# Attention scores from split operands, and the last two weight blocks in token order with the final norm on VectorE

## The chip, the cores and the metric

One NeuronCore of a Trainium2 chip runs the whole program in one launch. It has five engines with a queue each: TensorE (PE: matmuls; PEld: its weight loads), VectorE (DVE), ScalarE (ACT), GpSimd (POOL) and SyncE (SP, which here only issues transfers). The time is the device time of one execution in microseconds, given as the median of several runs.

## The reference

Two transformer layers over 1024 tokens of width 1024, all in float32. The first (`first_block`) mixes gated linear attention, a second recurrence and cross attention; the change doesn't touch it. The second (`second_block`) is where the change lies:

```python
h = x @ w_in[i]
ua, va, za, qh, kh, vh, zb, ga, gb = jnp.split(h, IN_OFFSETS, axis=-1)
...
q = apply_rope(qh.reshape(bn, s_len, B_HEADS, 2, B_QK_DIM), cos, sin) * (B_QK_DIM ** -0.5)
k = apply_rope(kh.reshape(bn, s_len, B_HEADS, 2, B_QK_DIM), cos, sin)
...
sc = jnp.einsum("bqhmd,bkhmd->bhmqk", qblk, k)          # 8 heads, 2 maps m, 64 wide
pr = jax.nn.softmax(jnp.where(mask, sc, -jnp.inf), axis=-1)
a = pr[:, :, 0] - lam * pr[:, :, 1]
o = jnp.einsum("bhqk,bkhd->bqhd", a, v)
...
merged = jax.nn.sigmoid(ga) * (ya @ w_branch_a[i]) + jax.nn.sigmoid(gb) * (yb @ w_branch_b[i])
mix_out = merged @ w_out[i]
x = layer_norm(DEEPNORM_ALPHA * x + mix_out + ple, ln_g[i], ln_b[i])
```

## The kernel before

The program is written by hand, engine by engine: each has a list of stages (`p0_..` to `p9_..`), and semaphores order the engines. Every large product is made from split operands: a value is stored as a high part (`at_hi`, `w_hi`, type float32r, a copy on ScalarE) and a low part (`at_lo`, `w_lo`, the difference, on VectorE or GpSimd), and three matmuls high x high, low x high, high x low add up in a PSUM bank. Weights come as 84 blocks of 256 columns; ScalarE makes `w_hi` of a block (`split_high`, line 390), GpSimd `w_lo` (`split_low`, line 377). A block has four tiles. In form F (lines 411 to 413) a tile is 128 features by 512 tokens, in form T (lines 422 to 424) it is two groups of 128 tokens by 256 columns, 48 matmuls. A quarter of a tile is a part (`gemm_part`).

The stages that matter here:

- Stage 5 ends with the rotation tables, the rotation of q (VectorE) and k (GpSimd) of head 0 in three steps each (`rope_third`), and the last block before the attention. All engines but TensorE then meet at `phase_end(5)`, which an engine leaves only when the others have come.
- Stage 8 is the differential attention, 8 heads with 8 query blocks of 128 tokens each (`head_pe`, `head_act`, `head_dve`, `head_pool`). For block qb TensorE computes the scores of block qb+1 in two PSUM areas, `ps_a` for map 0 and `ps_b` for map 1 (`attention_scores`, line 2480, keys in pieces of at most 512); VectorE adds the mask and takes the maximum (`scores_max`), ScalarE the exponential (line 2415), VectorE combines the maps into `da` (line 2277), TensorE transposes it (line 2447), ScalarE copies it to `daT` (line 2384), TensorE multiplies with v (line 2458). Between these steps TensorE works off 48 parts per head of other products, laid out in slots (`SLOT_PARTS`): 5 in `FIRST_SLOT`, 2 or 3 in front of the wait for `da`, and so on, 3 in `LAST_SLOT`. The first scores of the next head come behind the last product with v and before `LAST_SLOT` (`first_scores`). The scores are plain float32 products of the rotated q and k, map 0 on partitions 0 to 63 and map 1 on 64 to 127; q and k are double-buffered over heads (`dqx[head % 2]`), and SP loads those of the next head at the start of a head (`queries_load`). The rotation for the next head runs at query blocks 2 to 4.
- Stage 9 merges the branches and ends with `gemm_last`, two segments of two T blocks. Their tiles are added to `X` by VectorE (`sum_tile`, line 580, and `last_sum`, line 1774): block 0 for all four tiles (token pairs), then block 1. With the second segment's second block token pairs become complete one by one, and the final norm runs per group of 128 tokens: statistics of two halves (line 2844) and aggregation (line 2846) on VectorE, variance to 1/root on GpSimd (`root`, lines 300 and 302), the bias (line 2851) on VectorE, scale and bias on ScalarE (line 2792), gain on VectorE (line 2858), shift on GpSimd, or on VectorE for groups 5 and 7 (`last_shift`, line 2874), and the store by SP.

## Time and profile before

| | |
|---|---|
| time, median of 3 runs | 2433.26 us (2432.01 to 2437.83) |
| profiled execution | 2439.78 us, of it span 2437.9 us |
| TensorE busy | 2362.6 us, 97% |
| VectorE busy | 1290.5 us, 53% |
| ScalarE busy | 907.1 us, 37% |
| GpSimd busy | 792.2 us, 32% |
| TensorE's granted clock | full in nearly all slices |

The span runs from the first to the last recorded instruction. A matmul's recorded duration includes its way through the array, so records overlap; how fast TensorE works is read from the distance between two starts. The attention stage lies between 1372 and 2097 us of the span, the last block's tiles from 2366 us on.

### The profile page before, as it was taken

Reading aid. Unit: us, or ns where it says so; the run is one execution under the profiler, and the core shown is the slowest. Engines: PE = TensorE matmul, PEld = TensorE weight load, DVE = VectorE, ACT = ScalarE, POOL = GpSimd, SP = SyncE. Lnnn points to the kernel's source line nnn. Section 1 sums busy time; section 2 is a strip of 40 time slices with the busy share of each in tenths; the row PEclk is TensorE's granted clock in tenths of the full one; section 3 lists DMA queues with packets and bytes.
Section 4 is the critical chain, followed back from the end, with each engine's and each line's share of the span. In section 5 each row is a group of like instructions: output and inputs, shape, how many; then the busy total and the mean of one; then the engine's idle time right before and its main releaser. Section 6 shows DMA issues by size and latency. Waiting matters only on the chain.

```text
span 2437.9 us, 38783 instructions
## 1 busy us (share of the span) xinstructions
PE 2362.6 (97%) x15376; PEld 2042.5 (84%) x15376; DVE 1290.5 (53%) x2614; ACT 907.1 (37%) x1669; POOL 792.2 (32%) x712
## 2 busy tenths in 40 slices
PE   8999999999999999999999999999999999999995
PEld 7879978798788899999888898777898777887795
DVE  4002359999997433271323546446446446577626
ACT  4124554444444432242222333333333334544311
POOL 3111324445543221222443333233233232331123
PEclk9999999999999999999999999999999999999998
DMA  6234334443334522133334524314324314566611
GB/s 257 74 112 159 119 143 140 130 147 110 117 104 149 207 96 79 53 122 104 105 105 125 174 70 147 113 70 147 114 69 147 113 70 178 181 225 216 207 52 70
DMA packets 138940, 311.98 MB, mean 128 GB/s; under 512 B 12288, under 2 KB 55936, under 8 KB 127504
## 3 DMA queue, kind: packets, MB, share of 16 engines
q1 hardware_dynamic: 80080, 223.62, 26.8%
q10 hardware_dynamic: 58688, 86.00, 9.9%
q8 instruction: 116, 1.90, 0.3%
q14 instruction: 56, 0.46, 0.1%
HBM read 211.54 MB, written 98.04 MB: 127 GB/s over the span
## 4 chain that ended last, share of the span: by engine, by line
PE 86%; DVE 7%; issue 2%; POOL 1%; ACT 1%; DMA 1%; POOLq 0%; SPq 0%; ACTq 0%; DVEq 0%
PE bank L411 12%; PE bank L413 11%; PE bank L412 11%; PE bank L422 9%; PE bank L423 9%; PE bank L424 9%; PE bank L2480 3%; PE bank L2458 3%; PE bank L1842 3%; PE bank L1843 3%; PE bank L1841 3%; PE bank L1460 2%; PE bank L2447 1%; PE bank L730 1%; PE bank L2765 1%
## 5 line engine op out<-in xcount | busy, mean ns | idle before, releaser
L411 PE MATMUL bank<-at_hi,w_hi 128*128 128x512 f32 x1408 | 582.7, 414 | 2.6 <-DVE stage L2007 0.9
L422 PE MATMUL bank<-w_hi,at_hi 128*128 128x256 f32 x1920 | 556.8, 290 | 0.5 <-issue 0.5
L413 PE MATMUL bank<-at_hi,w_lo 128*128 128x512 f32 x1408 | 552.8, 393 | 0.0
L412 PE MATMUL bank<-at_lo,w_hi 128*128 128x512 f32 x1408 | 551.3, 392 | 0.0
L424 PE MATMUL bank<-w_hi,at_lo 128*128 128x256 f32 x1920 | 544.4, 284 | 0.0
L423 PE MATMUL bank<-w_lo,at_hi 128*128 128x256 f32 x1920 | 544.3, 283 | 0.0
L377 POOL TENSOR_TENSOR w_lo<-w_raw,w_hi 128x2048 fp32r<-128x2048 f32 x70 | 322.9, 4613 | 626.4 <-ACT w_hi L390 602.3
L422 PEld LDWEIGHTS bank<-w_hi,at_hi 128*128 128x128 f32 x1920 | 370.0, 193 | 13.2 <-issue 11.8
L423 PEld LDWEIGHTS bank<-w_lo,at_hi 128*128 128x128 f32 x1920 | 369.5, 192 | 0.7 <-issue 0.2
L424 PEld LDWEIGHTS bank<-w_hi,at_lo 128*128 128x128 f32 x1920 | 369.0, 192 | 0.0
L411 PEld LDWEIGHTS bank<-at_hi,w_hi 128*128 128x128 f32 x1408 | 268.9, 191 | 75.7 <-issue 23.3
L300 POOL TENSOR_TENSOR small<-small,cols 128x1 f32<-128x1 f32 (+1 forms) x162 | 54.9, 339 | 806.5 <-ACT da_junk L2399 439.4
L413 PEld LDWEIGHTS bank<-at_hi,w_lo 128*128 128x128 f32 x1408 | 265.5, 189 | 58.8
L412 PEld LDWEIGHTS bank<-at_lo,w_hi 128*128 128x128 f32 x1408 | 266.6, 189 | 51.9 <-issue 3.6
L447 ACT ACTIVATE stage<-bank 128x512 f32<-128x512 f32 x232 | 138.0, 595 | 441.4 <-PE bank L413 299.9
L390 ACT ACTIVATE w_hi<-w_raw 128x2048 fp32r<-128x2048 f32 x70 | 134.0, 1914 | 140.6 <-PE bank L424 104.9
L302 POOL TENSOR_TENSOR small<-small,cols 128x1 f32<-128x1 f32 (+1 forms) x162 | 146.5, 905 | 12.7
L2310 DVE SCALAR_TENSOR_TENSOR da_y<-bank,da_lam,da_gate 128x128 f32<-128x128 f32 x64 | 22.4, 350 | 236.5 <-PE bank L2468 236.5
L2384 ACT ACTIVATE da_aT<-bank 128x512 f32<-128x512 f32 (+2 forms) x96 | 47.1, 491 | 197.2 <-PE bank L2447 189.7
L2322 DVE TENSOR_REDUCE small<-bank 128x1 f32<-128x256 f32 (+7 forms) x128 | 97.1, 758 | 4.3
L2415 ACT ACTIVATE da_p<-bank,small 128x256 f32<-128x256 f32 (+7 forms) x128 | 93.2, 737 | 0.6 <-DVE small L2324 0.5
L1237 POOL TENSOR_TENSOR rec_z<-rec_z,rec_k 128x128 f32<-128x128 f32 x128 | 79.8, 624 | 25.9 <-ACT rec_z L1207 25.4
(300 smaller groups left out, 3606.7 us busy)
## 6 DMA issues: line engine op xcount, KB each, us to landing
w_raw<-in_weights SPq DMA_DIRECT2D x84, 1024.0 KB, 7.6
feat<-stage ACTq DMA_DIRECT2D x184, 256.0 KB, 2.0
tok<-stage ACTq DMA_DIRECT2D x72, 256.0 KB, 2.1
stage<-feat SPq DMA_DIRECT2D x32, 256.0 KB, 3.5
w_mem<-in_w_mem SPq DMA_DIRECT2D x4, 1024.0 KB, 7.5
x<-in_x SPq DMA_DIRECT2D x4, 1024.0 KB, 11.4
logg<-gate_g ACTq DMA_DIRECT2D x8, 512.0 KB, 2.8
rec_b<-logg SPq DMA_DIRECT2D x16, 256.0 KB, 5.1
```

Source lines behind the costliest of these rows:

```text
L302: pool.tensor_tensor(to, to, cols[:, ROOT:ROOT + 1].broadcast_to(shape), ALU.pow).then_inc(sem_, 1)
L377: pool.tensor_tensor(w_lo[b][:], w_raw[:, b, :, :], w_hi[b][:].bitcast(F32), ALU.subtract).then_inc(w_split, 1)
L390: nc.scalar.activation(w_hi[b][:], w_raw[:, b, :, :], ACT.Copy).then_inc(w_high, 1)
L411: nc.tensor.matmul(ps_gemm[i % 2], wh, ah, start=(k == 0), stop=False)
L412: nc.tensor.matmul(ps_gemm[i % 2], wh, al, start=False, stop=False)
L413: last = nc.tensor.matmul(ps_gemm[i % 2], wl, ah, start=False, stop=(k == KT - 1))
L422: nc.tensor.matmul(o, ah, wh, start=(k == 0), stop=False)
L423: nc.tensor.matmul(o, ah, wl, start=False, stop=False)
L424: last = nc.tensor.matmul(o, al, wh, start=False, stop=(k == KT - 1))
L447: nc.scalar.activation(stage[:, i, :], ps_gemm[i % 2], s.func, scale=s.scale).then_inc(tile_out, 1)
L2322: nc.vector.reduce_max(small[:, m:m + 1], flat, AX.X).then_inc(d_x, 1)
L2415: nc.scalar.activation(dp[:, m, 0:n], scored(ps, qb), ACT.Exp, bias=small[:, 2 + m:3 + m], scale=DSCALE, accum_out=small[:, 4 + m:5 + m]). ...
```

## The change

In the attention, q and k are split as the operands of the large products are. The rotated q and k are held once (`dqx`, `dkx`, no longer by head parity); ScalarE copies them to `dqh`, `dkh` (`queries_high`) and VectorE writes the differences `dql`, `dkl` (`queries_low`). For head 0 this is at the end of stage 5, for the others in query block 7 of the head before, behind ScalarE's last copies to `daT` and behind VectorE's norm of block 6. TensorE's first scores of a head, and SP's loads of the next q and k, wait for the differences. Head 0 runs its `FIRST_SLOT` ahead of its first scores. The scores of a piece of keys are six products: high x high, high x low, low x high, each for map 0 and then map 1.

At the end, the two blocks of the last segment are computed in the order of `LAST_TILES`, so that token pairs are finished one after another. The low part of the last weight block is made by VectorE. Statistics are taken over 256 columns, those of the first three quarters as soon as a pair's first tile is added. The norm is two VectorE passes: (x - mean) x gain, then x 1/root + shift; ScalarE's pass, the bias and GpSimd's shifts are gone.

```diff
         def queries_load(sp, head):
 
             row = head * P
-            if head >= 2:
-                sp.wait_ge(d_s, (head - 1) * 16 + 1)
             if head:
-                sp.wait_ge(d_rq, 3 * head)
-                sp.wait_ge(d_rk, 3 * head)
-            for x, swapped, at, done in ((dqx[head % 2], dqs, QF + row, d_in), (dkx[head % 2], dks, KF + row, d_in)):
+                sp.wait_ge(d_low, LOWS_BEFORE + 2 * head)
+            for x, swapped, at, done in ((dqx, dqs, QF + row, d_in), (dkx, dks, KF + row, d_in)):
...
+        def queries_high(act, head):
+
+            act.wait_ge(d_s, head * 16 + 1)
+            for hi, x, ready in ((dqh, dqx, d_rq), (dkh, dkx, d_rk)):
+                act.wait_ge(ready, 3 * head + 3)
+                nc.scalar.activation(hi[:], x[:], ACT.Copy).then_inc(d_high, 1)
+
+        def queries_low(dve, head):
+
+            for n, (lo, hi, x) in enumerate(((dql, dqh, dqx), (dkl, dkh, dkx))):
+                dve.wait_ge(d_high, HIGHS_BEFORE + 2 * head + n + 1)
+                nc.vector.tensor_tensor(lo[:], x[:], hi[:].bitcast(F32), ALU.subtract).then_inc(d_low, 1)
...
                     scores_max(dve, it, qb + 1)
+                elif not last_head:
+                    queries_low(dve, it + 1)
...
                     attention_exp(act, it, qb + 1)
+                elif it < B_HEADS - 1:
+                    queries_high(act, it + 1)
...
         def p8_pe(pe):
+            slot_products(pe, 0, FIRST_SLOT)
             first_scores(pe, 0)
...
         def first_scores(pe, it):
 
-            pe.wait_ge(d_rq, 3 * it + 3)
-            pe.wait_ge(d_rk, 3 * it + 3)
+            pe.wait_ge(d_low, LOWS_BEFORE + 2 * it + 2)
...
         def attention_scores(pe, it, qb):
             n = (qb + 1) * P
-            for m, ps in enumerate((ps_a, ps_b)):
-                if qb >= LONG:
-                    pe.wait_ge(d_e, it * 16 + (2 * qb + m + 1))
-                elif qb >= 2:
-                    pe.wait_ge(d_e, it * 16 + (2 * (qb - 1) + m + 1))
-                rows = slice(m * DK, (m + 1) * DK)
-                for a in range(0, n, HALF):
-                    w = min(HALF, n - a)
-                    last = nc.tensor.matmul(scored(ps, qb)[:, a:a + w], dqx[it % 2][rows, qb * P:(qb + 1) * P],
-                                            dkx[it % 2][rows, a:a + w],
-                                            start=True, stop=True)
-                last.then_inc(d_s, 1)
+            if qb >= LONG:
+                pe.wait_ge(d_e, it * 16 + (2 * qb + 2))
+            elif qb >= 2:
+                pe.wait_ge(d_e, it * 16 + (2 * (qb - 1) + 2))
+            for a in range(0, n, HALF):
+                w = min(HALF, n - a)
+                for i, (q, k) in enumerate(((dqh, dkh), (dqh, dkl), (dql, dkh))):
+                    for m, ps in enumerate((ps_a, ps_b)):
+                        rows = slice(m * DK, (m + 1) * DK)
+                        last = nc.tensor.matmul(scored(ps, qb)[:, a:a + w], q[rows, qb * P:(qb + 1) * P], k[rows, a:a + w],
+                                                start=(i == 0), stop=(i == 2))
+                        if i == 2 and a + w == n:
+                            last.then_inc(d_s, 1)
...
+            gemm_pe(pe, gemm_last[:1], lambda k, h: FILLED3 + (4 + h) * KT + k)
+            for n in range(len(LAST_TILES)):
+                last_tile(pe, n)
+
+        LAST_TILES = ((0, 0), (0, 1), (1, 0), (1, 1), (0, 2), (1, 2), (0, 3), (1, 3))
...
+            dve.wait_ge(w_split, gemm_last[1].first + 3)
+            split_low(dve, gemm_last[1].first // 2, 1)
+            for n, (b, i) in enumerate(LAST_TILES):
+                final_sum(dve, n)
+                for t in (2 * i, 2 * i + 1):
+                    if b:
+                        link(dve, statistics(t, 3))
+                        nc.vector.bn_aggr(lst[:, t, 0:2], lst[:, t, 4:28]).then_inc(l_var, 1)
+                    else:
+                        for part in range(3):
+                            statistics(t, part)
+                if b:
+                    for t in (2 * i, 2 * i + 1):
+                        centred(dve, t)
+                    for t in (2 * i, 2 * i + 1):
+                        normalized(dve, t)
...
+        def centred(dve, t):
+
             if t == 0:
                 dve.wait_ge(bc_in, 48)
-            nc.vector.tensor_tensor(X[:, t, :], X[:, t, :], bc[:, 0, :], ALU.mult).then_inc(l_g, 1)
+            dve.wait_ge(l_var, t + 1)
+            nc.vector.scalar_tensor_tensor(X[:, t, :], X[:, t, :], lst[:, t, 0:1], bc[:, 0, :], ALU.subtract,
+                                           ALU.mult).then_inc(l_g, 1)
+
+        def normalized(dve, t):
+
+            dve.wait_ge(l_g, t + 1)
+            dve.wait_ge(l_root, 2 * t + 2)
+            nc.vector.scalar_tensor_tensor(X[:, t, :], X[:, t, :], lst[:, t, 2:3], bc[:, 1, :], ALU.mult,
+                                           ALU.add).then_inc(l_out, 1)
```

## Rows read from the trace of the kernel before

**Rows 1.** The page: the span, and the chain that ended last by engine.

```profile
span 2437.9 us, 38783 instructions
PE 86%; DVE 7%; issue 2%; POOL 1%; ACT 1%; DMA 1%; POOLq 0%; SPq 0%; ACTq 0%; DVEq 0%
```

**Rows 2.** Timeline of the end: start, us, engine, line, count [idle before]; VectorE, then GpSimd.

```profile
2372.35 0.69 DVE L1774 TENSOR_TENSOR X<-bank,X 128x512 f32<-128x512 f32 x1 [5.07 <-PE bank L424]
...
2395.39 0.69 DVE L1774 TENSOR_TENSOR X<-bank,X 128x512 f32<-128x512 f32 x1 [5.07 <-PE bank L424]
2396.11 1.29 DVE L2844 BATCH_NORM_STATS2 lst<-X 128x6 f32<-128x512 f32 x2
2397.44 0.21 DVE L2846 BATCH_NORM_AGGREGATE lst<-lst 128x2 f32<-128x12 f32 x1
...
2418.91 0.68 DVE L1774 TENSOR_TENSOR X<-bank,X 128x512 f32<-128x512 f32 x1
...
2429.02 2.35 DVE L2858 TENSOR_TENSOR X<-X,bc 128x1024 f32<-128x1024 f32 x2
2431.40 3.25 DVE L2874 TENSOR_TENSOR X<-X,bc 128x1024 f32<-128x1024 f32 x1
...
2430.31 3.25 POOL L2874 TENSOR_TENSOR X<-X,bc 128x1024 f32<-128x1024 f32 x1 [3.62 <-DVE X L2858]
```

**Rows 3.** Timeline of a head's change and of three score blocks, TensorE and VectorE.

```profile
1640.81 1.95 PE L2458 MATMUL bank<-da_v,da_aT 128*128 128x128 f32 x16
1642.69 0.49 PE L2480 MATMUL bank<-da_k,da_q 64*128 64x128 f32 x4
...
1655.56 0.35 DVE L2277 SCALAR_TENSOR_TENSOR da_a<-da_p,small 128x128 f32<-128x128 f32 x1
...
1657.91 0.27 PE L2447 MATMUL bank<-ident,da_a 128*128 128x128 f32 x1
...
1668.44 1.13 PE L2480 MATMUL bank<-da_k,da_q 64*128 64x512 f32 x4
1669.50 0.50 PE L411 MATMUL bank<-at_hi,w_hi 128*128 128x512 f32 x1
...
1708.95 1.99 PE L2480 MATMUL bank<-da_k,da_q 64*128 64x512 f32 x8
1710.87 0.50 PE L411 MATMUL bank<-at_hi,w_hi 128*128 128x512 f32 x1
```

**Rows 4.** Timeline of TensorE where the attention stage begins.

```profile
1369.70 0.39 PE L411 MATMUL bank<-at_hi,w_hi 128*128 128x512 f32 x1
...
1371.52 0.39 PE L413 MATMUL bank<-at_hi,w_lo 128*128 128x512 f32 x1
...
1377.95 0.28 PE L424 MATMUL bank<-w_hi,at_lo 128*128 128x256 f32 x1
...
1379.76 0.28 PE L424 MATMUL bank<-w_hi,at_lo 128*128 128x256 f32 x1
...
1383.88 0.33 PE L2447 MATMUL bank<-ident,da_a 128*128 128x128 f32 x1
```

**Rows 5.** Timeline of ScalarE: two passes of 1024 columns, and a head's last copy.

```profile
1353.49 1.04 ACT L2357 ACTIVATE da_cos<-da_cos 128x1024 f32<-128x1024 f32 x1
1354.44 1.04 ACT L2357 ACTIVATE da_sin<-da_sin 128x1024 f32<-128x1024 f32 x1
...
1638.14 0.60 ACT L2384 ACTIVATE da_aT<-bank 128x512 f32<-128x512 f32 x1 [1.22 <-PE bank L2447]
```

**Rows 6.** Timeline of GpSimd and VectorE where the attention stage begins.

```profile
1374.99 4.62 POOL L377 TENSOR_TENSOR w_lo<-w_raw,w_hi 128x2048 fp32r<-128x2048 f32 x1 [7.68 <-ACT w_hi L390]
...
1379.71 0.30 DVE L2320 TENSOR_TENSOR bank<-bank,causal 128x128 f32<-128x128 f32 x1 [11.31 <-POOLq L290]
```

**Rows 7.** Stretches of TensorE around a fall of its clock: busy, granted clock, DMA share.

```profile
1026.00:1028.40 2.40, 1.73 (x12) 1.00 0.00 0
1028.40:1031.80 3.40, 3.40 (x18) 0.50 0.00 0
```

More of the change, by code:

```diff
@@ L216, in build @@
         with ExitStack() as own:
[L217 to L219 removed]
+            dqs, dks, dcos, dsin, dqx, dkx = [sb(f"da_{n}", [P, TOK], F32, own) for n in ("qs", "ks", "cos", "sin", "q", "k")]
+            dqh, dql, dkh, dkl = [sb(f"da_{n}", [P, TOK], F32R, own) for n in ("q_hi", "q_lo", "k_hi", "k_lo")]
             dv = [sb(f"da_v{n}", [P, NT, P], F32, own) for n in range(2)]
@@ L2768, in p9_pe, with last_tile @@
                     last.then_inc(e_prod, 1)
-            gemm_pe(pe, gemm_last, lambda k, h: FILLED3 + (4 + h) * KT + k)
+            gemm_pe(pe, gemm_last[:1], lambda k, h: FILLED3 + (4 + h) * KT + k)
+            for n in range(len(LAST_TILES)):
+                last_tile(pe, n)
+        LAST_TILES = ((0, 0), (0, 1), (1, 0), (1, 1), (0, 2), (1, 2), (0, 3), (1, 3))
+        def last_tile(pe, n):
+            g, (b, i) = gemm_last[1].first, LAST_TILES[n]
+            if i == 0:
+                pe.wait_ge(w_split, g + b + 3)
+            pe.wait_ge(tile_out, 4 * g + n + 1)
+            for j in range(2):
+                tok = slice((2 * i + j) * P, (2 * i + j + 1) * P)
+                o = ps_gemm[n % 2][:, j * CB:(j + 1) * CB]
+                for k in range(KT):
+                    wh, wl, ah, al = w_hi[b][:, k, :], w_lo[b][:, k, :], at_hi[:, k, tok], at_lo[:, k, tok]
+                    nc.tensor.matmul(o, ah, wh, start=(k == 0), stop=False)
+                    nc.tensor.matmul(o, ah, wl, start=False, stop=False)
+                    last = nc.tensor.matmul(o, al, wh, start=False, stop=(k == KT - 1))
+            last.then_inc(tile_done, 1)
         def p9_act(act):
@@ L2837, in merge, with final_sum, statistics @@
             nc.vector.scalar_tensor_tensor(x, x, ALPHA, e, ALU.mult, ALU.add).then_inc(e_out, 1)
-        POOL_SHIFTS = [t for t in range(NT) if t not in (NT - 3, NT - 1)]
-        def last_statistics(dve, t):
-            for n in range(2):
-                last = nc.vector.bn_stats(lst[:, t, 4 + 6 * n:10 + 6 * n], X[:, t, n * HALF:(n + 1) * HALF])
-            link(dve, last)
-            nc.vector.bn_aggr(lst[:, t, 0:2], lst[:, t, 4:16]).then_inc(l_var, 1)
-        def last_bias(dve, t):
-            dve.wait_ge(l_root, 2 * t + 2)
-            nc.vector.scalar_tensor_tensor(lst[:, t, 3:4], lst[:, t, 0:1], -1.0, lst[:, t, 2:3], ALU.mult,
-                                           ALU.mult).then_inc(l_nb, 1)
-        def last_gain(dve, t):
-            dve.wait_ge(l_x, t + 1)
+        def final_sum(dve, n):
+            g, (b, i) = gemm_last[1].first, LAST_TILES[n]
+            dve.wait_ge(tile_done, 4 * g + n + 9)
+            x = X[:, 2 * i:2 * i + 2, (2 + b) * CB:(3 + b) * CB]
+            nc.vector.tensor_tensor(x, ps_gemm[n % 2].rearrange("p (t n) -> p t n", t=2), x, ALU.add).then_inc(tile_out, 1)
+            dve.wait_ge(tile_out, 4 * g + n + 3)
+        def statistics(t, n):
+            return nc.vector.bn_stats(lst[:, t, 4 + 6 * n:10 + 6 * n], X[:, t, n * CB:(n + 1) * CB])
+        def centred(dve, t):
             if t == 0:
                 dve.wait_ge(bc_in, 48)
-            nc.vector.tensor_tensor(X[:, t, :], X[:, t, :], bc[:, 0, :], ALU.mult).then_inc(l_g, 1)
+            dve.wait_ge(l_var, t + 1)
[6 more added lines that the diff above has]
+                                           ALU.add).then_inc(l_out, 1)
         def p9_pool(pool):
             low_of(pool, gemm_a)
-            low_of(pool, gemm_last)
+            split_low(pool, gemm_last[1].first // 2, 0)
             for t in range(NT):
@@ L2865, in p9_pool @@
                 root(pool, lst[:, t, 2:3], lst[:, t, 1:2], E2, l_root, 2 * t + 1)
-                if t % 2 and t > 2:
-                    for before in (t - 3, t - 2):
-                        if before in POOL_SHIFTS:
-                            last_shift(pool, before, l_out)
-            last_shift(pool, NT - 2, l_out)
-        def last_shift(eng, t, done):
-            eng.wait_ge(l_g, t + 1)
-            eng.tensor_tensor(X[:, t, :], X[:, t, :], bc[:, 1, :], ALU.add).then_inc(done, 1)
         block = ctx.enter_context(nc.Block())
```

49 lines of the change are left out of this document (14 added, 35 removed).

## The prediction

> **What bounds the kernel now.** I read the page first. The chain that ended last is 86% TensorE and 7% VectorE, of a span of 2437.9 us [rows 1]. So almost everywhere a microsecond of TensorE's queue is a microsecond of time; the VectorE share has to be looked for in one place. The timeline of the last stretch shows where: TensorE's tiles of the last block arrive every 5.76 us (2372.35 to 2395.39 is four steps), so the eighth of them is due at 2412.67, but the span ends 25 us later. In between VectorE is behind: it takes the eighth tile only at 2418.91, and its last instruction ends at 2434.65 [rows 2]. Then I read TensorE's timeline around the scores, which are what the change rewrites there, and at last the places where the new instructions go: the start of the attention stage and the end of a head.
>
> **Part 1, the scores' products.** Before, each score product is a full f32 one and leaves two matmul records (four for two maps). For a block of queries with 512 and with 1024 keys, TensorE's next work starts 1.06 and 1.92 us after the first of them [rows 3]. That is 1.67 ns per key for both maps (0.86 us over 512 keys), or four columns' time at 2.4 GHz, plus a fixed 0.21. In the same stretch a full-array f32 product of 128 columns costs two records of 0.117 (16 in 1.88 us), also about four cycles per column, for one product. Two maps at the price of one: their products, on rows 0 to 63 and 64 to 127 of the array, already run side by side, although the program issues map 0 entirely before map 1. "The two maps in turn" therefore buys nothing that isn't there; what it must do is keep it.
>
> After, each piece of keys takes three passes of split operands per map instead of one f32 product. The price of such a pass is that of the other split products: 512 columns 0.2275 (1369.70 to 1371.52, eight steps), 256 columns 0.1207 (1377.95 to 1379.76, fifteen steps) [rows 4]; 384 columns lie between, 0.174. For 128 columns no row shows one. The f32 record of 128 columns takes 0.117, and the 256-column pass 0.1207, so I take 0.12. A head has pieces of 512 six times, and of 384, 256 and 128 twice each: 3 x (6 x 0.2275 + 2 x 0.174 + 2 x 0.1207 + 2 x 0.12) = 6.6 us. Before it was 4608 keys x 1.67 ns = 7.7. That is 1.1 a head, 8.8 us in eight. The side-by-side passes have less between them than the full-array ones (0.43 for 512 columns at two cycles each, which is 0.003 over the arithmetic, against 0.014 over it); with that the new passes cost 6.15, and the gain is 12.2. I take 10. The fixed 0.21 stays. No wait takes the gain back: at the block shown here VectorE's probabilities are ready at 1655.91 and TensorE transposes them at 1657.91 [rows 3], and the scores shorten a block by 0.36 us at most. The wait for both maps' exponentials instead of one is none, as both maps' passes already started together.
>
> **Part 2, the splits at a head's end.** ScalarE gets two copies of 1024 columns behind its last copy of transposed probabilities, VectorE two subtractions behind them, and TensorE's first scores of the next head wait for both. From rows: the copy ends at 1638.74, a ScalarE pass over 1024 columns takes 1.04 and the next starts 0.95 later, so the second ends at about 1640.8; a VectorE pass over 1024 takes 1.22 (two in 2.35), so the second difference ends at about 1642.3. TensorE's first score product began at 1642.69 [rows 3, 5]. I cost it at nothing, with a cover of 0.3 us: TensorE's products beside it. If the cover is missed by half a microsecond, seven heads cost 3.5, and by a whole VectorE pass 8.5. Behind the waiting instructions, ScalarE's eviction of a product tile moves by 1.2 us (its bank is next needed one tile, some 5 us, later), and VectorE's gate of the block before by about as much; TensorE asks for that only after its next three parts. The loads for the next head wait for the differences instead of the rotations, which end before the loads' place in SP's queue comes (behind the store of the head's outputs). The copies of q and k that are no longer double cost nothing for the same reason.
>
> **Part 3, the first head.** Here the cover is too short. ScalarE's weight split, for which GpSimd's w_lo pass waits, ends at 1374.9, the two new copies at about 1377. VectorE's differences then meet GpSimd's w_lo pass, 1374.99 to 1379.61 [rows 6]. Two such passes do not share: beside a GpSimd pass of 3.25 us a VectorE pass takes 3.25 where one alone takes 1.2, and ends when the other is done and its own 1.1 is over [rows 2]. So the differences run from 1379.6 to 1382.0. TensorE, with the first slot's five parts now ahead of the scores, starts them at 1371.75 and ends 60 x 0.1207 later, at 1379.0, and stands for 3 us. Before, VectorE began on the first scores when GpSimd was through the stage's end, at 1379.71, and TensorE's first transpose was at 1383.88, 4.17 later [rows 4, 6]. Now it begins at about 1382.6, and the transpose comes at 1386.8: +2.9 us. A standstill of this size may also drop the clock: in the rows at 1026 to 1032 TensorE has been busy 72% of the time before, and then runs 3.4 us at the 1.2 GHz level [rows 7]. That loses 1.7, of which the wait for the probabilities would hide some. I add 0.5. Bounds: +1.5 (the difference gets in before GpSimd) and +5.
>
> **Part 4, the end.** The order of the last eight tiles becomes (0,0) (0,1) (1,0) (1,1) (0,2) (1,2) (0,3) (1,3). A pair of token tiles is complete with its second block: at tiles 3, 4, 6 and 8, not 5 to 8. TensorE's work is the same; the second block's weights are wanted two tiles earlier, 11.5 us behind a split of 2048 columns, two passes of 1.04 on ScalarE and two of 1.14 on VectorE, so nothing waits. Statistics over 512 columns take 0.65 each (1.29 for two), over 256 I take 0.40 (between half and all of it). A first-block tile is 0.72 for the sum and six statistics, 2.9. A second-block tile is 0.72, two statistics and two aggregations (0.21 each) [rows 2] 1.2, and four passes over 1024 columns of 1.14: 6.5, with a wait for GpSimd's root behind VectorE's passes 6.75. Queue: tile 3 is due at 2383.87 and done at 2390.6, tile 4 at 2397.4, tile 5 at 2400.3, tile 6 (due 2401.15) at 2407.9, tile 7 at 2410.8, before tile 8 at 2412.67. So the end is 2412.67 + 6.75 = 2419.4, and with what follows VectorE's last instruction now (2437.9 - 2434.65 = 3.25, the last store), 2422.7. Gain 15.2 us. If the root holds up each pair by 1.1 and the short statistics cost as much as the long ones, VectorE is behind again and the gain is 10; with none of that 15.7. ScalarE's scaling and GpSimd's shift, whose passes now block VectorE's [rows 2], go away: they were part of the chain, not beside it.
>
> **Sum.** -10 - 15.2 + 2.9 + 0.5 = -21.8 us. The profiled execution took 2439.78 (span 2437.9 and 1.9 around it), 0.3% over the median of 2433.26; by its own time it becomes 2418.0, and the median 2411.5.
>
> **The rivals.** (a) Slower: the passes of the two maps don't run side by side at one column per cycle. All pairs in this trace do it at two cycles per column; at twice the rate both maps read and write together, which nothing here shows. Then each pair costs two passes: 13.2 us a head instead of 7.7, +44 in all, and the kernel ends at 2433.3 + 44 - 11.8 = 2465. It decides from the point where scores cost 12 us more than now, a pair at 1.4 passes. For it: no row. Against it: the exact four cycles per key. 6%.
>
> (b) Each pass shows its weight load. The fixed 0.21 says that a load is exposed where the array changes between its full and its split use; if half of it, 0.107, were paid at every pass, 36 passes a head would add 3.85 us to the 5.8 of their columns (three times 4608 at 2.4 GHz): 9.6 against 7.7, +15 in all, 2433.3 + 15.5 - 11.8 = 2437, no change. Against it: from 512 to 1024 keys two passes more cost 0.86, no load among them [rows 3]. 3%. The Trainium skill, "TensorE: Matmul & The Clock Gate", Part 3, says that weight loads overlap with matmuls in flight only when the row group differs; by that rule it would be this case, and the trace disagrees. The same page has matmuls start strictly in program order, under which the maps could not have overlapped before; the 1.67 ns per key disagree with that too.
>
> (c) Passes of 128 columns cost four cycles a column, 0.21 instead of 0.12: 48 of them, +4.6, 2416. Nothing in the trace speaks against it. 10%.
>
> (d) The splits at a head's end come late, by half to a whole VectorE pass in seven heads: 2415 to 2420. The cover is only 0.3 us. 13%.
>
> (e) VectorE stays behind at the end: gain 10, 2416.7. 8%.
>
> **Chances.** The forecast 60%. (c), (d) and (e) lie between 2415 and 2420, 31%; (a) 6%, (b) 3%. Range: forecast with gains of 8.8 to 12.2 and 13 to 15.7, a first head of +1.5 to +5, and the spread of the runs shown (2432.0 to 2437.8), reaches from 2405 to 2416; with (c) to (e) to 2421. A difference of 0.3%, 7.3 us, is about what can be told from no change here. Faster by more: 0.91; within: 0.03; slower: 0.06.
>
> **What would show it.** After: score blocks of 128, 512 and 1024 keys span about 0.57, 0.89 and 1.57 us; the first scores of head 0 start near 1382, those of the next heads directly behind the products before; VectorE's last tile is taken at its due time and the span ends 10 us behind the last matmul. The prediction is wrong if 512-key blocks take over 1.5 us (a), if TensorE stands before each head's first scores (d), or if the eighth tile waits for VectorE (e).

## The result, and the profile after

The changed kernel takes 2414.28 us (median; 2410.88 to 2414.99) against 2433.26: the ratio is 0.9917, with an interval of 0.9902 to 0.9932. Run once more on another chip it took 2412.51, a ratio of 0.9902 (0.9888 to 0.9915). The forecast was 2411.5. One execution of the kernel before took 5162.6 us and is in none of these numbers.

The page of the changed kernel: the span, the busy times, and the chain that ended last by engine, to be laid beside [rows 1].

```profile
span 2409.1 us, 39201 instructions
...
PE 2350.1 (98%) x15568; PEld 2055.7 (85%) x15568; DVE 1315.2 (55%) x2645; ACT 911.0 (38%) x1677; POOL 775.0 (32%) x705
...
PE 88%; DVE 8%; issue 1%; DMA 1%; ACT 1%; POOL 0%; ACTq 0%; DVEq 0%; SPq 0%
```

The spans of the two profiled executions differ by 28.8 us, more than the medians (19.0). 5.7 of it lies where both kernels are the same: the last product ahead of the attention starts at 1371.52 in the one and at 1365.85 in the other. That point moves from run to run, also in the kernels below (1360.4 to 1368.3), because short stretches at half clock fall now here, now there in the stages before: eight of them, 30.7 us in all, ahead of the attention in the run before, and four, 20.5 us in all, in the one after. Half of such a stretch is lost, so they account for some 5 of the 5.7. So I measure from it. From there to the end of the span it is 1066.4 us before, 1043.2 after, and 1043.9 in the other profiled run of the changed kernel. The change's own gain is 22.5 to 23.2 us. This table splits it; each number is a difference of two starts on TensorE, the last of a start and the span's end.

| stretch | before | after | difference | forecast |
|---|---|---|---|---|
| last product ahead of the attention to first transpose | 12.36 | 15.72 | +3.4 | +2.9 + 0.5 |
| first transpose to last product with v | 713.5 | 703.1 | -10.4 | -10 |
| from there to the last matmul | 315.0 | 314.2 | -0.8 | 0 |
| last matmul to the span's end | 25.56 | 10.25 | -15.3 | -15.2 |

**The scores.** TensorE's timeline in the changed kernel around score blocks of head 1: 128 keys (its first scores), 512 keys, the second piece (128 keys) of the block of 640, and 1024 keys. L2498 is the new scores; the row behind the blocks of 128, 512 and 1024 keys is TensorE's next work.

```profile
1457.46 0.33 PE L2498 MATMUL bank<-da_k_hi,da_q_hi 64*128 64x128 f32 x2
1457.62 0.27 PE L2498 MATMUL bank<-da_k_lo,da_q_hi 64*128 64x128 f32 x2
1457.73 0.27 PE L2498 MATMUL bank<-da_k_hi,da_q_lo 64*128 64x128 f32 x2
1457.94 0.39 PE L421 MATMUL bank<-w_hi,at_hi 128*128 128x256 f32 x1
...
1484.01 0.50 PE L2498 MATMUL bank<-da_k_hi,da_q_hi 64*128 64x512 f32 x2
...
1484.90 0.39 PE L421 MATMUL bank<-w_hi,at_hi 128*128 128x256 f32 x1
...
1492.70 0.23 PE L2498 MATMUL bank<-da_k_hi,da_q_hi 64*128 64x128 f32 x2
1492.76 0.28 PE L2498 MATMUL bank<-da_k_lo,da_q_hi 64*128 64x128 f32 x2
...
1523.84 0.49 PE L2498 MATMUL bank<-da_k_hi,da_q_hi 64*128 64x512 f32 x2
1524.17 0.39 PE L2498 MATMUL bank<-da_k_lo,da_q_hi 64*128 64x512 f32 x2
...
1525.42 0.51 PE L410 MATMUL bank<-at_hi,w_hi 128*128 128x512 f32 x1
```

The blocks span 0.48, 0.89 and 1.58 us; 512 and 1024 keys took 1.06 and 1.92 [rows 3]. Each row is a pair of passes, one for each map (x2), mostly 3 to 10 ns apart. Over the eight blocks of a head it is now 0.48, 0.55, 0.72, 0.90, 1.17, 1.24, 1.43, 1.59, sum 8.08 us; before it was 0.42, 0.63, 0.85, 1.06, 1.29, 1.50, 1.71, 1.92, sum 9.38. The difference, 1.30, is 10.4 us in eight heads.

**The first head.** The changed kernel at the start of the attention: timelines of ScalarE, GpSimd, VectorE, then TensorE, and then TensorE's granted clock in three stretches (busy, granted clock, DMA share).

```profile
1370.09 1.04 ACT L2187 ACTIVATE da_k_hi<-da_k 128x1024 fp32r<-128x1024 f32 x1
...
1369.32 4.63 POOL L376 TENSOR_TENSOR w_lo<-w_raw,w_hi 128x2048 fp32r<-128x2048 f32 x1 [8.13 <-ACT w_hi L389]
...
1370.22 4.81 DVE L2193 TENSOR_TENSOR da_q_lo<-da_q,da_q_hi 128x1024 fp32r<-128x1024 f32 x1 [7.94 <-ACT da_q_hi L2187]
1374.95 1.21 DVE L2193 TENSOR_TENSOR da_k_lo<-da_k,da_k_hi 128x1024 fp32r<-128x1024 f32 x1
1376.87 0.30 DVE L2333 TENSOR_TENSOR bank<-bank,causal 128x128 f32<-128x128 f32 x1 [0.71 <-PE bank L2498]
...
1376.22 0.33 PE L2498 MATMUL bank<-da_k_hi,da_q_hi 64*128 64x128 f32 x2 [2.31 <-DVE da_k_lo L2193]
...
1381.57 0.27 PE L2464 MATMUL bank<-ident,da_a 128*128 128x128 f32 x1
```

```profile
1374.00:1376.20 2.20, 0.00 (x0) 1.00 0.00 0
1376.20:1378.10 1.90, 1.88 (x20) 1.00 0.44 106
1378.10:1381.50 3.40, 3.40 (x18) 0.50 1.04 296
```

VectorE's first difference is ready to run at 1370.22, but GpSimd has been in its weight pass since 1369.32. The difference is recorded at 4.81 us instead of 1.2 and ends 1.08 behind GpSimd's end (1373.95). The second follows, and TensorE stands 2.3 us. TensorE does nothing from 1374.0 to 1376.2, works for 1.9 us at full clock, and then for 3.4 us at half clock (1.2 GHz), as in the rows at 1028 [rows 7].

**A head's end.** ScalarE and VectorE in the changed kernel, the end of head 0.

```profile
1452.79 0.60 ACT L2398 ACTIVATE da_aT<-bank 128x512 f32<-128x512 f32 x1 [1.26 <-PE bank L2464]
1453.29 1.05 ACT L2187 ACTIVATE da_q_hi<-da_q 128x1024 fp32r<-128x1024 f32 x1
1454.23 1.05 ACT L2187 ACTIVATE da_k_hi<-da_k 128x1024 fp32r<-128x1024 f32 x1
...
1455.51 1.22 DVE L2193 TENSOR_TENSOR da_k_lo<-da_k,da_k_hi 128x1024 fp32r<-128x1024 f32 x1
```

The second difference ends at 1456.73, 0.73 us ahead of TensorE's first scores (1457.46). The distance from TensorE's last product with v to these scores is 0.205, as before, in all seven heads: nothing stands.

**The end.** VectorE and GpSimd from the last-but-one tile on, and TensorE's last matmul, in the changed kernel.

```profile
2394.32 0.68 DVE L2876 TENSOR_TENSOR X<-bank,X 128x512 f32<-128x512 f32 x1
2395.03 2.06 DVE L2881 BATCH_NORM_STATS2 lst<-X 128x6 f32<-128x256 f32 x6
2399.16 0.69 DVE L2876 TENSOR_TENSOR X<-bank,X 128x512 f32<-128x512 f32 x1 [2.07 <-PE bank L2803]
...
2401.11 2.41 DVE L2888 SCALAR_TENSOR_TENSOR X<-X,lst,bc 128x1024 f32<-128x1024 f32 x2
2403.44 2.48 DVE L2895 SCALAR_TENSOR_TENSOR X<-X,lst,bc 128x1024 f32<-128x1024 f32 x2
...
2402.45 1.48 POOL L301 TENSOR_TENSOR lst<-lst,cols 128x1 f32<-128x1 f32 x1
...
2398.84 0.28 PE L2803 MATMUL bank<-w_hi,at_lo 128*128 128x256 f32 x1
```

VectorE has been idle for 2.07 us when the last tile comes; before, it took its last tile 6.2 us late [rows 2]. From there it needs 6.75 us (2399.16 to 2405.91), and the store 3.2 more: 10.0 us from taking the last tile to the end, where it was 19.0 (2418.91 to 2437.9). So of the 15.3 us some 6 are the lateness and 9 the work behind the last tile. In the kernel before, the tile taken at 2410.07 kept VectorE for 8.85 us, and its longest part is an operation on one column per partition:

```profile
2415.57 2.29 DVE L2851 SCALAR_TENSOR_TENSOR lst<-lst 128x1 f32<-128x1 f32 x1 [0.71 <-POOL lst L302]
```

This is the bias. It takes 0.11 where GpSimd is idle (at 2413.62), and here it ends with GpSimd's shift pass (2415.50 to 2417.84). The new norm has neither.

### The profile page after: what moved, and what is told of

It is laid out like the page before. It is cut to its first block, busy times and chain, and to the rows that moved or that the text cites. A ratio compares the mean times of both kernels' runs of the same rounds, so it can differ in the third digit from the quotient of the medians.

```text
span 2409.1 us, 39201 instructions
## 1 busy us (share of the span) xinstructions
PE 2350.1 (98%) x15568; PEld 2055.7 (85%) x15568; DVE 1315.2 (55%) x2645; ACT 911.0 (38%) x1677; POOL 775.0 (32%) x705
## 3 DMA queue, kind: packets, MB, share of 16 engines
q8 instruction: 117, 1.92, 0.3%
## 4 chain that ended last, share of the span: by engine, by line
PE 88%; DVE 8%; issue 1%; DMA 1%; ACT 1%; POOL 0%; ACTq 0%; DVEq 0%; SPq 0%
PE bank L410 12%; PE bank L412 12%; PE bank L411 12%; PE bank L421 9%; PE bank L422 8%; PE bank L423 8%; PE bank L2498 3%; PE bank L2475 3%; PE bank L1841 3%; PE bank L1840 3%; PE bank L1842 3%; PE bank L2464 1%; PE bank L1459 1%; PE bank L729 1%; PE bank L2780 1%
## 5 line engine op out<-in xcount | busy, mean ns | idle before, releaser
L421 PE MATMUL bank<-w_hi,at_hi 128*128 128x256 f32 x1792 | 521.1, 291 | 0.8 <-issue 0.8
L423 PE MATMUL bank<-w_hi,at_lo 128*128 128x256 f32 x1792 | 508.8, 284 | 0.0
L422 PE MATMUL bank<-w_lo,at_hi 128*128 128x256 f32 x1792 | 508.6, 284 | 0.0
L421 PEld LDWEIGHTS bank<-w_hi,at_hi 128*128 128x128 f32 x1792 | 345.9, 193 | 8.9 <-issue 7.1
L422 PEld LDWEIGHTS bank<-w_lo,at_hi 128*128 128x128 f32 x1792 | 345.6, 193 | 0.7 <-issue 0.2
L423 PEld LDWEIGHTS bank<-w_hi,at_lo 128*128 128x128 f32 x1792 | 345.1, 193 | 0.0
L410 PEld LDWEIGHTS bank<-at_hi,w_hi 128*128 128x128 f32 x1408 | 268.0, 190 | 64.7 <-issue 12.5
L299 POOL TENSOR_TENSOR small<-small,cols 128x1 f32<-128x1 f32 (+1 forms) x162 | 52.7, 326 | 795.6 <-ACT da_junk L2415 431.4
L301 POOL TENSOR_TENSOR small<-small,cols 128x1 f32<-128x1 f32 (+1 forms) x162 | 124.1, 766 | 12.7
L1236 POOL TENSOR_TENSOR rec_z<-rec_z,rec_k 128x128 f32<-128x128 f32 x128 | 95.2, 744 | 26.4 <-ACT rec_z L1206 26.0
```

The lines of the kernel that those rows point to most:

```text
L301: pool.tensor_tensor(to, to, cols[:, ROOT:ROOT + 1].broadcast_to(shape), ALU.pow).then_inc(sem_, 1)
L410: nc.tensor.matmul(ps_gemm[i % 2], wh, ah, start=(k == 0), stop=False)
L421: nc.tensor.matmul(o, ah, wh, start=(k == 0), stop=False)
L422: nc.tensor.matmul(o, ah, wl, start=False, stop=False)
L423: last = nc.tensor.matmul(o, al, wh, start=False, stop=(k == KT - 1))
L1236: eng.tensor_tensor(z1, z1, k1, ALU.mult)
```

## The experiments

Times are medians. "Changed" means the kernel after the change. Stretches are read as in the table above. The intervals of the changed kernel's own two ratios reach from 0.9888 to 0.9932. Experiments 4 and 7 to 10 have ratios within them, so the times alone don't tell these kernels from the changed one, and only the stretches show what each does.

**1. Only the scores' part.** The edit undoes everything in the last stage; these are its main lines:

```diff
-            gemm_pe(pe, gemm_last[:1], lambda k, h: FILLED3 + (4 + h) * KT + k)
-            for n in range(len(LAST_TILES)):
-                last_tile(pe, n)
+            gemm_pe(pe, gemm_last, lambda k, h: FILLED3 + (4 + h) * KT + k)
...
-                    for t in (2 * i, 2 * i + 1):
-                        centred(dve, t)
-                    for t in (2 * i, 2 * i + 1):
-                        normalized(dve, t)
```

> The kernel before with the change's scores alone: split operands, passes of the maps in turn, the first slot ahead of head 0's scores; the end is that of before. My theory (parts add up): 10.3 us less in the attention, 3.4 us more at head 0, so 7 us less than before, about 2426.5; 25.5 us from the last matmul to the end as before. Rival (the parts interact, or the scores' gain is given back by the end): within 3 us of before.

2425.0 us, ratio 0.9973 (0.996 to 0.9986) to the kernel before (2431.93 on this chip): -7. First transpose to last product with v takes 702.9 us, and last matmul to end 25.6, as before the change.

**2. Only the end.** The reverse: the attention is that of the kernel before.

```diff
-            pe.wait_ge(d_low, LOWS_BEFORE + 2 * it + 2)
+            pe.wait_ge(d_rq, 3 * it + 3)
+            pe.wait_ge(d_rk, 3 * it + 3)
...
-            slot_products(pe, 0, FIRST_SLOT)
```

> The kernel before with the change's end alone. My theory: the last matmul to the end goes from 25.6 us to 10.3, the attention is as before, so 15.3 us less, about 2418. Together with the scores alone it gives the whole change, 22 us. Rival: the end's gain depends on when weights or constants arrive, and is under 12 us without the earlier attention.

2418.72 us, ratio 0.9934 (0.9914 to 0.9954), or -13. The trace gives the size better: last matmul to end takes 10.25 us (-15.3), the attention's stretch 713.8. The two parts are additive: -7 and -13 timed make 20, and the two traces give -10.6 for the attention's stretch, +2.8 ahead of it and -15.3, which is -23.1.

**3. The two maps one after the other.**

```diff
-            for a in range(0, n, HALF):
-                w = min(HALF, n - a)
-                for i, (q, k) in enumerate(((dqh, dkh), (dqh, dkl), (dql, dkh))):
-                    for m, ps in enumerate((ps_a, ps_b)):
-                        rows = slice(m * DK, (m + 1) * DK)
+            for m, ps in enumerate((ps_a, ps_b)):
+                rows = slice(m * DK, (m + 1) * DK)
+                for a in range(0, n, HALF):
+                    w = min(HALF, n - a)
+                    for i, (q, k) in enumerate(((dqh, dkh), (dqh, dkl), (dql, dkh))):
```

> The changed kernel, but each block's scores are issued with all of map 0's passes first and then all of map 1's. My theory: TensorE runs the two row halves side by side whatever the order of issue (the f32 scores of before, issued map by map, cost 1.67 ns per key for both), so score blocks span the same 0.48, 0.90 and 1.59 us and the time is that of the changed kernel within 3 us. Rival (matmuls start in the order of issue, so that the alternation is what brings the overlap): with a block's three or six passes of a map in a row only one neighbouring pair overlaps; a 512-key block goes from 0.90 to about 1.35 us or more, a head from 8.1 us of scores to about 13, and the time is 35 to 45 us longer, about 2455.

2430.35 us, ratio 0.9987 (0.9977 to 0.9996). Neither theory gave this. Blocks of up to 512 keys are unchanged (0.90 for 512); those of two pieces take 1.74, 1.82, 2.00 and 2.18 instead of 1.17 to 1.59, and the stretch of the attention is 722.0 us, 18.9 longer. TensorE's timeline of a block of 1024 keys in this kernel:

```profile
1529.95 0.50 PE L2498 MATMUL bank<-da_k_hi,da_q_hi 64*128 64x512 f32 x1
1530.30 0.40 PE L2498 MATMUL bank<-da_k_lo,da_q_hi 64*128 64x512 f32 x1
1530.54 0.39 PE L2498 MATMUL bank<-da_k_hi,da_q_lo 64*128 64x512 f32 x1
1530.54 0.62 PE L2498 MATMUL bank<-da_k_hi,da_q_hi 64*128 64x512 f32 x2
...
1531.58 0.39 PE L2498 MATMUL bank<-da_k_lo,da_q_hi 64*128 64x512 f32 x1
1531.81 0.39 PE L2498 MATMUL bank<-da_k_hi,da_q_lo 64*128 64x512 f32 x1
1532.14 0.50 PE L410 MATMUL bank<-at_hi,w_hi 128*128 128x512 f32 x1
```

The first two passes run alone. The third (high k, low q) has a high x high pass beside it, 7 ns later. It is 0.228 ahead of the next one of map 0, so it must be on the other half of the rows: map 1's first, the seventh in TensorE's queue. It starts when the third does and did not start with the first or second. At the other end map 1's last two passes (from 1531.58 on) run alone. So TensorE starts a pass ahead of its turn: from four places ahead (the seventh with the third), but not from five or six (with the second or the first). It is the same in all 32 blocks of two pieces: the seventh pass starts 0.57 to 0.59 us behind the first. As the first three passes are 512 columns wide in all of them, no run here tells a reach counted in places from one counted in time.

The Trainium skill, "TensorE: Matmul & The Clock Gate", Part 3, says that matmuls start in program order without exception; the trace disagrees, as the seventh starts 0.23 us ahead of the fourth. The same section says that small products on distinct groups of rows start about 4 ns apart; here the distances are mostly 3 to 10 ns.

**4. The maps apart within each piece.** If the reach is four places, nothing should be lost with the maps three passes apart instead of six.

```diff
-                for i, (q, k) in enumerate(((dqh, dkh), (dqh, dkl), (dql, dkh))):
-                    for m, ps in enumerate((ps_a, ps_b)):
-                        rows = slice(m * DK, (m + 1) * DK)
+                for m, ps in enumerate((ps_a, ps_b)):
+                    rows = slice(m * DK, (m + 1) * DK)
+                    for i, (q, k) in enumerate(((dqh, dkh), (dqh, dkl), (dql, dkh))):
```

> The changed kernel, but within each piece of keys map 0's three passes come first and then map 1's three. With the maps apart over the whole block (six passes each where there are two pieces) blocks of over 512 keys went from 1.59 to 2.18 us, those of one piece (three passes each) did not. My theory: TensorE starts a pass of the other row half ahead of its turn if it stands at most four places behind the passes in progress; here it stands three behind, so all blocks span what they do in the changed kernel (0.90 and 1.59 us for 512 and 1024 keys), and the time is within 3 us of it. Rival (what matters is that the two pieces differ in bank, or that a second piece cannot start ahead of the first): blocks of two pieces stay at about 2.2 us and the time at about 2430.

2410.01 us, ratio 0.9901 (0.9886 to 0.9916); the changed kernel on the same chip has 0.9902. The attention's stretch is 703.7 us. A block of 1024 keys in this kernel:

```profile
1518.47 0.50 PE L2498 MATMUL bank<-da_k_hi,da_q_hi 64*128 64x512 f32 x2
1518.81 0.40 PE L2498 MATMUL bank<-da_k_lo,da_q_hi 64*128 64x512 f32 x2
...
1520.07 0.51 PE L410 MATMUL bank<-at_hi,w_hi 128*128 128x512 f32 x1
```

All are pairs again and the block spans 1.59. Map 1's first pass, the fourth in the queue, starts 10 ns behind the first. Three places ahead is in reach, four is by experiment 3, and five isn't.

**5. The kernel before, with its maps in turn.** The old f32 products, two per map, are issued piece by piece.

```diff
-            for m, ps in enumerate((ps_a, ps_b)):
...
-                for a in range(0, n, HALF):
-                    w = min(HALF, n - a)
+            for a in range(0, n, HALF):
+                w = min(HALF, n - a)
+                for m, ps in enumerate((ps_a, ps_b)):
```

> The kernel before, with its plain f32 score products issued in turn for the two maps within each piece of keys, and the wait for both maps' exponentials in front, as in the change. My theory: an f32 product is two passes, so map by map the other map's first pass stands at most four behind, and all of it already overlaps: no change, within 3 us of before, blocks of 1024 keys at 1.92 us. Rival (the wait for both exponentials costs something, or the turn gains something for f32 too): over 3 us either way.

2435.53 us, ratio 1.0003 (0.9993 to 1.0013), and blocks of 0.42 to 1.92 us as before. In the kernel before, map 1's first product was the third in the queue at most. It leaves two records to a product, so its first record is the fifth, four places behind the first, and starts 13 to 14 ns after it. By either count that is within the reach of experiment 3: turns buy nothing there.

**6. The splits at a head's end one tile later.**

```diff
-                elif it < B_HEADS - 1:
-                    queries_high(act, it + 1)
...
+                if it < B_HEADS - 1 and qb == NT - 1:
+                    queries_high(act, it + 1)
```

> The changed kernel with ScalarE's two split copies of a head's end issued after the eviction of the product tile instead of before it, about 1.3 us later. In the changed kernel the second difference ends 0.73 us before the next head's first scores start. My theory: the cover is about 0.5 to 0.7 us, so TensorE stands 0.6 to 0.8 us before the first scores of seven heads, 4 to 6 us in all, about 2419. Rival (the wait is covered more widely, TensorE's queue hides it): no change within 2 us.

2421.15 us, ratio 0.9948 (0.993 to 0.9966). The attention's stretch is 713.4 us: the whole gain of the scores is gone. ScalarE at the end of head 0 in this kernel, then TensorE's first scores of head 1:

```profile
1452.33 0.60 ACT L2398 ACTIVATE da_aT<-bank 128x512 f32<-128x512 f32 x1 [1.27 <-PE bank L2464]
1453.76 0.60 ACT L446 ACTIVATE stage<-bank 128x512 f32<-128x512 f32 x1 [0.84 <-PE bank L423]
1454.39 0.37 ACTq L456 DMA_DIRECT2D tok<-stage  x1
1455.16 1.06 ACT L2187 ACTIVATE da_q_hi<-da_q 128x1024 fp32r<-128x1024 f32 x1 [0.80 <-ACT stage L446]
...
1458.66 0.33 PE L2498 MATMUL bank<-da_k_hi,da_q_hi 64*128 64x128 f32 x2 [1.60 <-DVE da_k_lo L2193]
```

The copies begin 2.83 us behind the start of the last copy to `daT`, where they began 0.50 behind it. The eviction is not 0.6 us of work but a wait for the tile (0.84), the pass, and 0.80 from the pass's end to the next pass, in which the transfer is issued (0.37). The first scores then start 1.59 us behind the last product with v (1.87 in head 1, for which this row stands) instead of 0.205. 2.3 later costs 1.4 per head: the cover was 0.9 us.

**7. The first head's high parts ahead of the last weight split.**

```diff
                 for i in range(4):
                     evacuate(act, s, 0, b, i)
+                    if (b, i) == (1, 2):
+                        queries_high(act, 0)
...
-            queries_high(act, 0)
```

> The changed kernel with ScalarE's copies of head 0's q and k issued two evictions earlier, right behind the rotation, so that VectorE's differences are over before GpSimd's last w_lo pass of the stage begins. TensorE's first slot still stands ahead of the scores. My theory (the standstill at head 0 comes from VectorE's difference waiting for GpSimd's pass): TensorE's gap of 2.6 us before the first scores goes, and with it the 3.4 us at half clock; from the last product of the stage before to the first transpose it takes 13.6 to 14.5 us instead of 15.7, as VectorE still takes the scores only after the stage's end; time 1.5 to 2 us less, about 2412.5. Rival (the cause is the stage's end, or the order of ScalarE's queue): the gap stays.

2411.14 us, ratio 0.9915 (0.99 to 0.993; the kernel before had 2432.63 on this chip). VectorE and GpSimd in this kernel:

```profile
1364.59 1.22 DVE L2193 TENSOR_TENSOR da_q_lo<-da_q,da_q_hi 128x1024 fp32r<-128x1024 f32 x1 [1.19 <-ACT da_q_hi L2187]
1365.73 1.22 DVE L2193 TENSOR_TENSOR da_k_lo<-da_k,da_k_hi 128x1024 fp32r<-128x1024 f32 x1
...
1369.86 4.61 POOL L376 TENSOR_TENSOR w_lo<-w_raw,w_hi 128x2048 fp32r<-128x2048 f32 x1 [7.54 <-ACT w_hi L389]
```

Ahead of GpSimd's pass both differences take 1.22 each. TensorE doesn't stand (gap of 0.21), its clock stays full, and the last product to the first transpose takes 12.8 us instead of 15.7, less than the 13.6 expected. From VectorE's first score pass to the transpose it is 4.17 us, as before the change, against 4.70 in the changed kernel, so 0.5 of the changed kernel's 3.4 us are clock; experiments 1, 3 and 9, without the fall of the clock, have 15.2. From 15.2 to 12.8, 2.4 us, is the price of meeting GpSimd. The 0.5 that are left against 12.36 come from the first slot: TensorE starts the scores only behind it, 8.0 us after the last product, and VectorE gets them at 8.65, where it began at 8.19 in the kernel before.

**8. The same, with the first scores ahead of `FIRST_SLOT` again.**

```diff
         def p8_pe(pe):
-            slot_products(pe, 0, FIRST_SLOT)
             first_scores(pe, 0)
```

> The same with head 0's first scores ahead of the first slot again, as in the kernel before. My theory: the first transpose comes 12.3 us after the last product of the stage before, as in the kernel before (12.36), so 3.4 us less than the changed kernel: about 2411. Rival: ScalarE's early copies delay the eviction of a tile and TensorE stands for them, no gain.

2410.24 us, ratio 0.9914 (0.99 to 0.9928). The stretch is 12.5 us, with a gap of 1.08 in front of the scores, as the second difference ends late (1366.62). In experiment 10, which starts the attention the same way, it ends in time, the gap is 0.65 as in the kernel before, and the stretch 12.35. Against experiment 7 the order of slot and scores is worth 0.3 to 0.5 us by the traces; the timed runs can't tell them apart.

**9. The old order of the last tiles, with the new norm.**

```diff
-        LAST_TILES = ((0, 0), (0, 1), (1, 0), (1, 1), (0, 2), (1, 2), (0, 3), (1, 3))
+        LAST_TILES = ((0, 0), (0, 1), (0, 2), (0, 3), (1, 0), (1, 1), (1, 2), (1, 3))
```

> The changed kernel with its new norm, but the last eight tiles in the order of before: all four tiles of the first block, then all four of the second. It parts the end's gain of 15.3 us. My theory: VectorE needs 6.65 us for each second-block tile that comes every 5.76, so it falls behind by 0.9 a tile: the last tile is taken 2.7 us late, 13.0 us from the last matmul to the end instead of 10.3. So 12.6 us of the gain belong to the norm in two passes without ScalarE and GpSimd, and 2.7 to the order; time about 2417. Rival (the order is what matters): over 18 us from the last matmul to the end, about 2422 or more.

2412.28 us, ratio 0.992 (0.9904 to 0.9935), and not the 2417 expected: timed, no different from the changed kernel. In the trace last matmul to end is 12.97 us. VectorE in this kernel, the last two tiles:

```profile
2393.75 0.68 DVE L2876 TENSOR_TENSOR X<-bank,X 128x512 f32<-128x512 f32 x1
...
2400.41 0.68 DVE L2876 TENSOR_TENSOR X<-bank,X 128x512 f32<-128x512 f32 x1
```

A tile that completes a pair costs VectorE 6.66 us, TensorE delivers one in 5.76, and three of them in a row put VectorE 3 x 0.9 = 2.7 us behind. So of the end's 15.3 us 2.7 come from the order and 12.6 from the rest of the end's change: the norm in two passes, without ScalarE's and GpSimd's parts, and the statistics taken early. No run here splits the 12.6 further.

**10. The last tile in two halves**, with the edits of 7 and 8. Each group of 128 tokens of the last tile gets a bank and a signal of its own.

```diff
+                if j and n == len(LAST_TILES) - 1:
+                    o = ps_fill[1][:, 0:CB]
...
-            last.then_inc(tile_done, 1)
+                if j or n == len(LAST_TILES) - 1:
+                    last.then_inc(tile_done, 1)
```

> The early splits with the scores first, and the last tile handed over in its two token groups, each in a bank of its own, so that VectorE normalizes group 6 while TensorE still computes group 7. My theory: from the last matmul to the end it takes 7.8 us instead of 10.3, another 2.4 us: about 2408.5, the fastest version. Rival (the tail is the last store and GpSimd's root, which stay): under 1 us.

2408.04 us, ratio 0.9898 (0.9884 to 0.9913), the lowest median here, though its interval overlaps that of the changed kernel. But last matmul to end falls only to 9.79, not 7.8. VectorE in this kernel:

```profile
2392.23 2.06 DVE L2893 BATCH_NORM_STATS2 lst<-X 128x6 f32<-128x256 f32 x6
2394.20 0.41 DVE L2857 TENSOR_TENSOR X<-bank,X 128x256 f32<-128x256 f32 x1
...
2397.23 1.28 DVE L2907 SCALAR_TENSOR_TENSOR X<-X,lst,bc 128x1024 f32<-128x1024 f32 x1 [0.51 <-POOL lst L301]
2398.43 0.42 DVE L2857 TENSOR_TENSOR X<-bank,X 128x256 f32<-128x256 f32 x1
```

The first half is taken directly behind the six statistics of the tile before, with no idle time, and the second 2.1 us after its last matmul ends (2396.31): VectorE has become the bound. And with one group at a time nothing covers GpSimd's root, which costs 0.51 per group; with pairs the second group's pass covered it.

The remaining run was the changed kernel beside experiments 4 and 5:

> The changed kernel itself, for a comparison on the same chip as the variants of this call. 2411 to 2415; first transpose 15 to 16 us after the last product of the stage before, 10.3 us from the last matmul to the end, 703 us from the first transpose to the last product with v.

It gave 2412.51 us and blocks of 0.48 to 1.60.

## Why the prediction was right, and where it wasn't

**Part 1, the scores** (-10 forecast, -10.4 in the stretch, -10.4 by the blocks). The step from rows was sound for pieces of 256 keys and more: a pair of passes on half the rows each costs what one full-array pass of the same width does. 512 columns are 0.23, 384 are 0.175 and 256 are 0.12. Rival (a) is dead by these numbers, and so is (b), which would put 0.32 us between passes of 512 columns. So is (c): passes of 128 columns are 0.11 apart (1457.62 to 1457.73), not 0.21. What the fixed 0.21 of a block is, no run here shows.

The 10 came out so near to 10.4 partly by luck. The sum from rows was 8.8. Between it and 12.2 the prediction chose 10, on the ground that passes side by side have less between them than full-array ones (0.003 us over the columns' time). They don't: the pairs of 512 columns are 0.23 apart, 0.017 over it. Nor does the 6.15 a head behind the 12.2 follow from that ground, which gives 5.9, or 6.25 with 0.12 for 128 columns; without the fixed parts it measured 6.4. What lifted the gain over 8.8 was the width for which there was no row. Without the fixed 0.21 three passes of 128 columns cost 0.27 us (a block of 128 keys takes 0.48; 0.57 was forecast), where three times 0.12 had been taken; in a block of 640 keys the first of them takes 0.06 (1492.70 to 1492.76). That is 0.17 a head, 1.4 us in eight, of the 1.6 between 8.8 and 10.4.

Another argument of this part was wrong: "'The two maps in turn' therefore buys nothing that isn't there". It was drawn from a program with two products per map, and holds for that (experiment 5). With six passes per map it does not: issued map after map, the new scores would have cost 18.9 us more (experiment 3), and the attention's stretch would be 8.5 us longer than before (722.0 against 713.5). I inferred that the maps run side by side whatever the order of issue, without asking from how far ahead.

**Part 2, head ends** (0 forecast, 0 measured). The cover was given as 0.3 us; the trace has 0.73, and experiment 6 about 0.9. ScalarE starts its next pass 0.1 us ahead of the recorded end of the one before, which the step that added whole records from 1638.74 on left out. The price of missing it was right in kind: 9.7 us for seven heads in experiment 6. Rival (d) begins at 0.7 to 0.9 us of delay, not at 0.3, so its 13% were too many.

**Part 3, the first head** (+2.9 and +0.5 forecast, +3.4 measured). Each step stands in the trace: the difference that doesn't share with GpSimd's pass, the stand of TensorE, the half clock after it. The runs without the fall of the clock (experiments 1, 3 and 9, 15.2 us) separate the two terms: 0.5 is the clock and 2.8 the rest (2.9 forecast). Of the 2.8, experiment 7 gives 2.4 to meeting GpSimd and 0.5 to the first slot ahead of the scores. The clock's fall turned out to be one that comes in some profiled runs and not in others with the same program at this place (last section), so that its 0.5 was in the trace is luck. The Trainium skill, "SBUF — State Buffer", section "SBUF: two separate sides", says that of a VectorE pass with two SBUF inputs and a GpSimd pass that reads SBUF the first holds the port for its whole duration and the other waits; the 4.81 us beside 4.63 agree.

**Part 4, the end** (-15.2 forecast, -15.3 measured). The queue was right: VectorE takes the last tile when it is due and needs 6.75 us, the number forecast. Its terms were not all exact: statistics of 256 columns are 0.43 for a single one and 0.34 in a row (0.40 taken), an aggregation is 0.27 (0.21 taken), and the six statistics with their sum 2.8 (2.9). The forecast's 0.25 for a wait for GpSimd's root isn't there: the root of the second group is ready at 2403.93, ahead of the pass that needs it (2404.63). Instead the four passes take 1.20 each, not 1.14. The errors cancel, so the exact 6.75 is luck, and the shape of the queue is not. Rival (e) is dead by the 2.07 us of idle time, and experiment 9 shows what falling behind would have been worth with the old order: 2.7 us.

**The sum.** -21.8 was forecast and -22.5 to -23.2 measured in the stretches that the change touches. The timed difference is 19.0 in the first comparison and 20.6 in the second. Runs of one kernel spread over up to 12 us (2426.48 to 2438.82 in 19 runs of the kernel before), which is why the terms were told apart in the traces. The 0.8 us between the attention and the last tiles is no more than runs differ: in the thirteen profiled runs this stretch takes 314.1 to 315.0 us, with 315.0 both in kernels that have the change's scores and in those that don't.

## What to carry to other kernels

Here independent products on different halves of the array's rows ran side by side only if the partner was within about four matmuls in the queue, so issue them in turn once each is made of several passes. Before moving a step past "one eviction" count its wait for the product and the issue of its transfer: here 0.6 us of work were 2.3 us of delay. At a kernel's end compare the time per tile of the finishing engine with that of the producer (8.85 before, 6.66 after, against 5.76): with the new norm the order of the tiles was worth 0.9 us for each of the three that would come in a row, and the rest of the end's change 12.6.

## What the runs showed of the hardware

- TensorE starts a matmul ahead of its turn if its rows are free. Three places ahead is in reach (full pairing in experiment 4, with 10 ns between partners) and so is four (the third pass runs with the seventh in experiment 3), five is not; or the limit is one of time, which no run here rules out. Issued map after map, a block of 1024 keys takes 2.18 us instead of 1.59.
- A tiny GpSimd operation on one column per partition is held up by VectorE's two-source passes, and a tiny VectorE operation by GpSimd's: `root` (L301) takes 0.55 us when it finds VectorE in its short operations, and 1.40 to 1.48 beside a pass over 1024 columns; in the kernel before VectorE's bias (L2851) takes 0.11, and 2.29 beside GpSimd's shift pass.
- TensorE's stand of 2.3 us at the start of the attention, the same in all kernels with the splits there, was followed by 3.4 us at the 1.2 GHz level in four profiled runs (the changed kernel twice, experiments 4 and 6) and by none in three (experiments 1, 3 and 9). The stretch from first scores to first transpose took 5.35 us with it and 4.82 without. What decides between them the runs do not show.
